# Six heads a layer turned by VectorE and a DRAM round trip in place of TensorE transposes, in a two-layer MLA and differential-attention trunk

## The reference

```python
h = rms_norm(r, norm_mix_pre[layer])
proj = h @ w_in[layer]        # q_lat, kv_lat, k_pe, dq, dk, dv, g_a, g_b
# branch A: 8 MLA heads, keys and queries 64 + 32 wide, values 64 wide
p = softmax(causal(qa @ ka.T * mla_scale))      # per head, float32
out_a = (p @ va) @ w_o_mla[layer]
# branch B: 4 differential heads, two maps each, values 128 wide
p = softmax(causal(q1 @ k1.T)) - lam * softmax(causal(q2 @ k2.T))
out_b = (rms_norm(p @ vd, diff_subln) * (1 - lam_init)) @ w_o_diff[layer]
mix = (sigmoid(g_a) * out_a + sigmoid(g_b) * out_b) @ w_out[layer]
r = r + rms_norm(mix, norm_mix_post[layer])
# then a SwiGLU feed-forward with 2,816 hidden columns, and r = r + rms_norm(ff)
```

## Time and profile before

| | |
|---|---|
| Time of three runs | 797.07 us median (796.63 to 797.28) |
| Profiled execution | 796.88 us, span 795.1 us |
| TensorE matmul busy | 787.6 us, 99% |
| VectorE, ScalarE, GpSimd busy | 575.2, 452.1, 135.8 us |
| `transposes`, L1602 | 120 matmuls, median record 273 ns |
| Attention stretches | about 94 to 158 us and 492 to 557 us of the span |

### The profile page before, as it was taken

The page is one execution under the profiler, slowest core; times in us unless marked ns, Lnnn a source line. Parts: engine busy times, 40 slices in busy tenths (PEclk is TensorE's granted clock), DMA queues, the critical chain, the costliest instruction groups (busy, mean ns, idle before and its releaser), DMA issues.

```text
span 795.1 us, 16819 instructions
## 1 busy us (share of the span) xinstructions
PE 787.6 (99%) x6300; PEld 763.7 (96%) x6300; DVE 575.2 (72%) x964; ACT 452.1 (57%) x766; POOL 135.8 (17%) x146
## 2 busy tenths in 40 slices
PE   9999999999999999999999999999999999999997
PEld 9999899999999999999999999999999999999885
DVE  6899787686787666766668987976867977676432
ACT  6657665674565444455557467566755754544331
POOL 0212000233421111101122202000433211111000
PEclk9999999999999999999999999999999999999999
DMA  9767333355266555355654674334652766657951
GB/s 335 260 219 240 129 108 105 108 182 162 57 202 216 165 169 174 119 165 169 195 174 134 197 239 149 107 106 133 181 168 77 220 212 183 193 175 197 274 134 53
DMA packets 55531, 134.87 MB, mean 170 GB/s; under 512 B 20896, under 2 KB 21536, under 8 KB 55344
## 3 DMA queue, kind: packets, MB, share of 16 engines
q1 hardware_dynamic: 38608, 131.43, 52.5%
q10 hardware_dynamic: 16864, 2.62, 1.9%
HBM read 131.93 MB, written 2.10 MB: 169 GB/s over the span
## 4 chain that ended last, share of the span: by engine, by line
PE 98%; DMA 0%; DVE 0%; ACT 0%; issue 0%; DVEq 0%
PE bank L1327 25%; PE bank L1329 24%; PE bank L1328 24%; PE bank L1361 4%; PE bank L1748 3%; PE bank L1749 3%; PE bank L1747 3%; PE bank L1352 2%; PE bank L1602 2%; PE bank L1571 2%; PE bank L1621 1%; PE bank L1420 1%; PE bank L1573 1%; PE bank L1377 1%; PE bank L1576 1%; PE bank L1381 1%
## 5 line engine op out<-in xcount | busy, mean ns | idle before, releaser
L880 DVE TENSOR_TENSOR w_lo<-w_raw,w_hi 128x1024 fp32r<-128x1024 f32 x246 | 331.0, 1348 | 37.7 <-ACT w_hi L436 34.3
L1327 PE MATMUL bank<-h_hi,w_hi 128*128 128x272 f32 (+1 forms) x1200 | 346.0, 288 | 0.0
L1329 PE MATMUL bank<-h_hi,w_lo 128*128 128x272 f32 (+1 forms) x1200 | 342.8, 286 | 0.0
L1328 PE MATMUL bank<-h_lo,w_hi 128*128 128x272 f32 (+1 forms) x1200 | 341.9, 285 | 0.0
L436 ACT ACTIVATE w_hi<-w_raw 128x1024 fp32r<-128x1024 f32 x246 | 258.9, 1056 | 121.5 <-PE bank L1329 56.4
L1327 PEld LDWEIGHTS bank<-h_hi,w_hi 128*128 128x128 f32 x1200 | 226.2, 189 | 0.5
L1329 PEld LDWEIGHTS bank<-h_hi,w_lo 128*128 128x128 f32 x1200 | 226.2, 189 | 0.0
L1328 PEld LDWEIGHTS bank<-h_lo,w_hi 128*128 128x128 f32 x1200 | 226.0, 188 | 0.0
L845 POOL TENSOR_TENSOR pbuf<-sbuf,ubuf 128x272 f32<-128x272 f32 (+1 forms) x44 | 38.4, 874 | 205.6 <-DVE ubuf L1257 204.0
L778 POOL TENSOR_TENSOR acc<-acc,sq 128x272 f32<-128x272 f32 (+1 forms) x45 | 47.5, 1055 | 137.0 <-ACT sq L449 136.8
L1257 DVE TENSOR_TENSOR ubuf<-bank,rstd_h 128x272 f32<-128x272 f32 (+1 forms) x44 | 18.9, 431 | 44.8 <-PE bank L1329 44.8
(11 more groups left out here) (238 smaller groups left out, 1234.7 us busy)
## 6 DMA issues: line engine op xcount, KB each, us to landing
w_raw<-weights SPq DMA_DIRECT2D x216, 512.0 KB, 4.0
w_raw<-weights SPq DMA_DIRECT2D x16, 384.0 KB, 3.6
w_raw<-weights SPq DMA_DIRECT2D x16, 320.0 KB, 2.9
w_first<-first_weights SPq DMA_DIRECT2D x2, 512.0 KB, 7.6
x_tok<-x_rows SPq DMA_DIRECT2D x1, 1024.0 KB, 11.3
turn<-y ACTq DMA_DIRECT2D x4, 256.0 KB, 7.2
r_tok<-turn ACTq DMA_DIRECT2D x8, 128.0 KB, 5.6
out_tokens<-o_tok SPq DMA_DIRECT2D x4, 256.0 KB, 2.0
```

Of the source, the lines that this page charges most:

```text
L880: dve.tensor_tensor(w_lo[:, n % RING, :], w_raw[:, n % RAW, :], w_hi[:, n % RING, :].bitcast(f32), ALU.subtract).then_inc(lo_ready, 1)
L1327: pe.matmul(dst, wh, hi, start=first, stop=False)
L1328: pe.matmul(dst, wh, lo, start=False, stop=False)
L1329: return pe.matmul(dst, wl, hi, start=False, stop=last)
```

## The change

`MOVED` names units 4 to 9. Their probabilities no longer go through TensorE. VectorE turns every 32 x 32 block of the 416 columns into `e_second`, right behind `probs(u)`. SP sends this in four DMAs (one for each group of 32 partitions, in pieces of 128 bytes) to the DRAM tensor `moved`, in such an order that its rows are keys and its columns queries. One unit later SP fetches what it needs in two DMAs with rows of 512 bytes into a buffer (`pt_a`, `pt_b0`, `pt_b1`: four for the units in flight), and two units later ScalarE's queue fetches the two narrow edges of 16 x 16. GpSimd zeroes the edge columns once a layer. TensorE's product of units 4 and 5 runs in step 8 in place of 6, that of 6 and 7 in step 10 in place of 8, that of 8 and 9 in `first_output_tiles`, with the halves of each handled by `hi_out` and `out_part` one step later than their product. Units 0 to 3, 10 and 11 are still transposed by TensorE.

The core of the diff:

```diff
+MOVED = range(DIFF_HEADS, UNITS - 2)
+SENDS = 4
+FETCHES = 2
@@ SP
+                def send_probs(u):
+                    sp.wait_ge(probs_turned, moved_to(l, u))
+                    to = moved_rows(l, u).rearrange("(b k) q -> k b q", k=32)
+                    for g in range(4):
+                        sp.dma_start(to[:, :, 32 * g:32 * g + 32], e_second[32 * g:32 * g + 32, u % 2, :].rearrange("p (b q) -> p b q", q=32)).then_inc(probs_sent[u % 2], 16)
+
+                def fetch_probs(u):
+                    if u == MOVED[0]:
+                        sp.wait_ge(edges_padded, l + 1)
+                    if u >= MOVED[0] + 4:
+                        sp.wait_ge(pv_ready, PRODUCTS * l + products_to(u - 4))
+                    if moved_to(l, u) > 1:
+                        sp.wait_ge(probs_landed, 16 * FETCHES * (moved_to(l, u) - 1))
+                    sp.wait_ge(probs_sent[u % 2], 16 * SENDS * pair_moved_to(l, u))
+                    p, rows = probs_of(u), moved_rows(l, u)
+                    sp.dma_start(p[:, N_META + T_B0:].rearrange("p (c q) -> p c q", c=2)[:, :, 0:P], rows[B0:B0 + 2 * P, :].rearrange("(c k) q -> k c q", c=2)).then_inc(probs_landed, 16)
+                    sp.dma_start(p[:, N_META + T_A0:N_META + T_A0 + P], rows[A0:A0 + P, :]).then_inc(probs_landed, 16)
...
+                for u in MOVED:
+                    load(at + u - MOVED[0], SLOT)
+                    send_probs(u)
+                    if u > MOVED[0]:
+                        fetch_probs(u - 1)
+                fetch_probs(MOVED[-1])
@@ ScalarE
                 def exps(u):
+                    if u - 2 in MOVED:
+                        act.wait_ge(probs_turned, moved_to(l, u - 2))
...
+                def fetch_edges(u):
...
+                    act.wait_ge(probs_sent[u % 2], 16 * SENDS * pair_moved_to(l, u))
+                    for at, row in ((T_A1, A0 + P), (T_B2, B0 + 2 * P)):
+                        act.dma_start(probs_of(u)[0:16, N_META + at:N_META + at + 16], moved_rows(l, u)[row:row + 16, P - 16:]).then_inc(edges_landed, 16)
+
                 def pt_evac(u):
-                    act.wait_ge(pt_ready, UNITS * l + u + 1)
+                    if u in MOVED:
+                        return
+                    act.wait_ge(pt_ready, turned_to(l, u))
...
-                    if u >= 2:
+                    if 2 <= u < DIFF_HEADS + 2:
                         hi_out(u - 2)
+                    elif u - 4 in MOVED:
+                        hi_out(u - 4)
                     split(S("gate") + i + HI_AHEAD)
+                    if u - 2 in MOVED:
+                        fetch_edges(u - 2)
...
+                hi_out(MOVED[-1])
                 pt_evac(UNITS - 1)
@@ VectorE
+                        if u in MOVED:
+                            after(v)
+                            dve.wait_ge(probs_ready, UNITS * l + u + 1)
+                            if u - 2 in MOVED:
+                                dve.wait_ge(probs_sent[u % 2], 16 * SENDS * pair_moved_to(l, u - 2))
+                            dve.transpose(e_second[:, u % 2, :], e[:, 0:A1]).then_inc(probs_turned, 1)
...
-                    if u >= 2:
-                        out_part(u - 2)
+                    if u - 4 in MOVED:
+                        out_part(u - 4)
...
                 dve.transpose(head_rstd[:, 0:32 * n].rearrange("p (b j) -> p b j", j=32), head_rec[:, 0:n, None].to_broadcast([P, n, 32])).then_inc(norm_bc, 1)
+                out_part(MOVED[-1])
                 out_part(UNITS - 1)
@@ TensorE
                 def pv(u):
-                    pe.wait_ge(pt_copied, UNITS * l + u + 1)
-                    if not ends_product(u):
-                        return
+                    if u in MOVED:
+                        pe.wait_ge(probs_landed, 16 * FETCHES * moved_to(l, u))
+                        pe.wait_ge(edges_landed, 16 * 2 * moved_to(l, u))
+                    else:
+                        pe.wait_ge(pt_copied, turned_to(l, u))
...
-                        if u:
+                        if 0 < u <= DIFF_HEADS:
                             pv(u - 1)
+                        elif u - 3 in MOVED and ends_product(u - 3):
+                            pv(u - 3)
                         if u == UNITS - 2:
                             head_sums()
-                        transposes(u)
+                        if u not in MOVED:
+                            transposes(u)
...
-                    for k in range(3):
+                    for k in range(2):
                         heads_ready(k)
                         for m in range(2):
                             chunk(m, k)
-                    pv(UNITS - 1)
+                    pv(MOVED[-1])
                     slot_ready(S("oa") + 1)
                     bank_free(TL("oa") + 2)
-                    for k in range(3):
+                    for k in range(2):
                         chunk(2, k)
-                    heads_ready(3)
-                    for m in range(3):
-                        chunk(m, 3)
+                    pv(UNITS - 1)
+                    for k in range(2, 4):
+                        heads_ready(k)
+                        for m in range(3):
+                            chunk(m, k)
```

More of the change, by code:

```diff
@@ L69, in first_map, with moved_to, pair_moved_to, turned_to @@
     return 2 * u if u < DIFF_HEADS else u + DIFF_HEADS
+MOVED = range(DIFF_HEADS, UNITS - 2)
+SENDS = 4
+FETCHES = 2
+def moved_to(l, u):
+    return len(MOVED) * l + u - MOVED[0] + 1
+def pair_moved_to(l, u):
+    return len(MOVED) // 2 * l + (u - MOVED[0]) // 2 + 1
+def turned_to(l, u):
+    return (UNITS - len(MOVED)) * l + (u if u < MOVED[0] else u - len(MOVED)) + 1
 def products_to(u):
@@ L240, in build_trunk @@
         (b_t,), at = place(at, [("b_t", [P, 4, TOK], f32)])
+        (pt_a,), _ = place(base + 4 * ((RAW + 2 * RING) * SLOT + GAIN_COLS + 4 * KC * TOK + 6 * TOK), [("pt_a", [P, 2, N_META + PT_COLS], f32)])
+        (pt_b0,), _ = place(lat_at + 4 * (2 * E_COLS + 2 * (N_META + PT_COLS) + 16 * UNITS), [("pt_b0", [P, N_META + PT_COLS], f32)])
+        assert _ <= lat_at + 4 * 10 * TOK
+        (pt_b1,), _ = place(lat_tmp_at + 4 * TOK, [("pt_b1", [P, N_META + PT_COLS], f32)])
+        moved = nc.dram_tensor("moved", (DEPTH * len(MOVED) * A1, P), f32).ap()
         (pm,), _ = place(lat_tmp_at, [("pm", [16, 3, 256], f32)])
@@ L315, in build_trunk @@
         probs_first = sem("probs_first")
+        probs_turned, probs_landed, edges_landed, edges_padded = (sem(n) for n in ("probs_turned", "probs_landed", "edges_landed", "edges_padded"))
+        probs_sent = [sem(f"probs_sent{i}") for i in range(2)]
         scores_ready, negmax_ready, exp_ready, probs_ready = (sem(n) for n in ("scores_ready", "negmax_ready", "exp_ready", "probs_ready"))
@@ L353, in maps_of, with probs_of, moved_rows @@
             return [(4 + u % 2, e_t[:, u % 2, :], 0)]
+        def probs_of(u):
+            if u not in MOVED:
+                return pt[:, u % 2, :]
+            return pt_a[:, u % 2, :] if (u - MOVED[0]) // 2 % 2 == 0 else (pt_b0, pt_b1)[u % 2][:, :]
+        def moved_rows(l, u):
+            return moved[(moved_to(l, u) - 1) * A1:moved_to(l, u) * A1, :]
         def T0(l):
@@ L397, in _ @@
                 end = d0 if l < DEPTH - 1 else plan.slots
+                def send_probs(u):
[14 more added lines that the diff above has]
+                    sp.dma_start(p[:, N_META + T_A0:N_META + T_A0 + P], rows[A0:A0 + P, :]).then_inc(probs_landed, 16)
+                at = plan.slot[l, "gate", 14] + MOVED[0]
+                whole = (at - first) // RING
+                with sp.Fori(0, whole) as i:
+                    for j in range(RING):
+                        load(first + j, SLOT, i, RING)
+                for n in range(first + whole * RING, at):
+                    load(n, SLOT)
+                for u in MOVED:
[4 more added lines that the diff above has]
+                fetch_probs(MOVED[-1])
+                first = at + len(MOVED)
                 whole = (end - first) // RING
@@ L471, in latent @@
                 if l and i == 0:
-                    act.wait_ge(pt_ready, UNITS * l)
+                    act.wait_ge(pt_ready, turned_to(0, UNITS - 1))
+                    act.wait_ge(probs_landed, 16 * FETCHES * moved_to(0, MOVED[-1]))
                 square(K, i if i < QC else i - QC, ps[bank_of(t)][:, c0:TOK], c0)
@@ L606, in hi_out @@
                     act.activation(am_hi[:, (u - DIFF_HEADS) // 2, t0:], ps[7][:, t0:TOK], ACT.Copy).then_inc(out_hi, 1)
+                def fetch_edges(u):
+                    if u == MOVED[0]:
+                        act.wait_ge(edges_padded, l + 1)
+                    if u >= MOVED[0] + 4:
+                        act.wait_ge(pv_ready, PRODUCTS * l + products_to(u - 4))
+                    if moved_to(l, u) > 1:
+                        act.wait_ge(edges_landed, 16 * 2 * (moved_to(l, u) - 1))
+                    act.wait_ge(probs_sent[u % 2], 16 * SENDS * pair_moved_to(l, u))
```

(32 more changed lines are left out.)

## The result

| | before | after |
|---|---|---|
| Median of 13 executions each | 796.92 us | 798.59 us |
| Lowest to highest | 796.46 to 797.48 | 796.98 to 801.55 |
| Profiled execution, its span | 796.88, 795.1 | 797.03, 795.1 |
| Mean granted clock | 0.998 in the profiled one (0.998 to 1.000 in 42 later executions) | 0.993 to 0.999 |

The ratio of the times is 1.003, 95% interval 1.0019 to 1.0041: slower, by 1.7 us at the median. The forecast was 0.3 us faster (796.6 us, 794.1 to 799.9). The median isn't the whole result. The kernel before stays within 1.0 us. The one after takes 797.0 us at best, and its times come in bunches near 798.4, 800.4 and 801.5 us, each with a lower mean clock.

A forecast was written before the change was run, and what follows sets the result against it. TensorE, busy 99% of the span, was taken to bound the kernel. Spared work, pauses and waits (-6.0 + 4.7 + 0.8 = -0.5 us) gave 796.4 us, the median 0.2 higher at 796.6 us, range 794.1 to 799.9.

The forecast's parts named there:

- TensorE spared: Attention stretch: sixty transposes go from TensorE, saving 3.0 us a layer, 6.0 us in all, up to 6.4 us.
- The pause: Ahead of the product of units 10 and 11, TensorE waits for `out_part(9)`: 2.3 us a layer, 4.7 us in all.
- VectorE's turn: Turning a 416-wide block, behind the unit's probabilities and ahead of the gate copy: 0.60 us, bounds 0.45 and 1.25 us.
- The wait at scores 8: TensorE waits for the exponentials of unit 7: 0.2 us in layer 0, 0.6 us in layer 1, together 0.8 us.
- The round trip hidden: Sends to and fetches from `moved` for unit 9, layer 1, need 8.7 us of 10.1 us before product 9.
- the late case: Rival: the round trip makes product 9 wait up to 4 us in layer 1; 804.1 us at middle values, chance 0.12.
- The sum: TensorE spared, pause and scores wait: -6.0 + 4.7 + 0.8 = -0.5 us on the profiled 796.88 us, giving 796.4.
- the clock's fall: Rival: TensorE's clock falls in the pause, 2.3 us a layer; 798.9 us for one, 801.2 for both, chance 0.12.

The follow-up runs named there:

- the long kernel: Kernel after, with one more VectorE reduction over 832 columns, its result unused, ahead of `out_part(9)`: 802.07 us, ratio 1.0067 against the kernel before.
- fill: Kernel after, with 34 small matmuls, their result unread, on TensorE ahead of the last value product: 797.06 us, ratio 1.000 against the kernel before.

## Why the prediction was wrong, step by step

- **TensorE spared, 6.0 us**: 5.6 by the table above. Right within 0.4 us.
- **The pause, 2.3 us a layer by the string root, reciprocal, wide transpose, `out_part(9)`**: right in mechanism, place and size. From product 9 to the last product was to be 159.32 - 155.10 = 4.22 us and is 155.69 - 151.49 = 4.20 us. Idle is 2.25 us and 2.2 to 2.3 us. Moving `out_part(9)` takes all of it away, which shows that the order in VectorE's queue, not the work, is the cause.
- **VectorE's turn, 0.60 us**: 0.61 us. **The wait at scores 8, 0.8 us**: 1.0 us, and the reduction in step 6 carries most of it, since its move gives 0.7 us back. The terms given for it make 10.8 - 10.1 = 0.7 us and 0.7 - 3 x 0.2 = 0.1 us where the text says 0.6 and 0.2; the sum is the same.
- **The round trip hidden**: right. TensorE never waits for it. A send was taken at 0.33 us to issue and 3.5 us to land and took 0.48 and 2.9 us at the median. The price of the late case was misread, though: the 2.9 and 6.0 us of the earlier trace rows mix the 128-byte sends into `turn` with the fetches out of it. The page of before has them apart, and with 7.2 us for the sending leg the late case would have come out 1.2 us dearer:

```profile
turn<-y ACTq DMA_DIRECT2D x4, 256.0 KB, 7.2
r_tok<-turn ACTq DMA_DIRECT2D x8, 128.0 KB, 5.6
```

  The Trainium skill wants pieces of 512 B and more for line rate ("DMA: Bandwidth & Descriptors", Specifications). Sends in 128-byte pieces cost TensorE nothing here; no run has the same sends in larger pieces, so what the small pieces cost them isn't shown.
- **The sum, -0.5 us against the profiled execution**: an execution without a fall takes 797.03 us, 0.15 us above the profiled one of before, 0.6 us off. This part of the forecast stands.
- **The failing step: the clock's fall counted at nothing in the sum, with a chance of 0.12.** It was set aside because the clock outlasts TensorE's work by 2.9 us at the end of the kernel and the pause is 2.3 us. That comparison was the error, in two ways.

A pause need not last until the fall. In the profile with one fall, TensorE's last matmul ahead of the pause ended near 153.4 and the clock fell near 156.1, 2.7 us later, when TensorE had been back at work since 155.7. Behind the pause of layer 1 in the kernel before with a pause it is 2.7 us too (557.3, 560.0), again with TensorE back at work since 559.6.

One instance at the end of the kernel was read as a limit, and it varies. In the long kernel the fall comes 3.1 us after the last matmul in layer 0 and 4.5 us in layer 1, there 1.3 us after TensorE resumed. At the end of the twelve profiled executions it comes 2.6 to 4.8 us after the last matmul. The longest is that of fill, whose matmuls end at 789.8 (columns as in the earlier trace rows):

```profile
793.00:794.00 1.00, 0.00 (x0) 0.00 (x0) 0.00 (x0) 0.00 (x0) 0.00 (x0) 1.00 1.03 383
794.00:795.00 1.00, 0.00 (x0) 0.00 (x0) 0.00 (x0) 0.00 (x0) 0.00 (x0) 0.79 0.34 127
```

Of 27 executions of the kernel after, 20 have a mean clock of 0.996 or less, the value of the profiled one with a fall, and 7 have 0.998 or more. So the rival's chance was far too low. Its price was too high: 2.3 us a fall, for 18 matmuls at the lower level, where the level came back after 3.4 us and the fall cost 1.6. With two places a kernel and 1.6 us each, the forecast would have been 798.2 us with one fall and 799.8 us with both. The median, 798.59 us, lies between the two, and its clock, 0.996, is that of one fall.

The Trainium skill ("TensorE: Matmul & The Clock Gate", What's actually happening) says that the gate's timing doesn't start anew with a kernel, and that this is why the point where the clock changes varies from run to run. The traces agree in that it varies: of two profiled executions with the same start of the product and the same 2.25 us of pause, one has a fall and one hasn't. That the cause is the one the page gives, no run here shows.

What stays open: which of the two layers falls how often; why the kernel before with its pause of 2.3 us fell in four executions of four, where the kernel after stayed up in 7 of 27; and the bunch at 801.4 to 801.6 us, 4.5 us above the undisturbed one, which is more than two falls of 1.6 us. Its mean clock, 0.993, is lower as well than the 0.994 or 0.995 of the bunch near 800.4, so the clock has a part in it, but no profile of it was taken.

## What to carry to other kernels

Before a producer is moved later, look in its engine's queue at what stands between it and the instruction that frees the consumer's buffer: here a 1.3 us transpose and what it waits for stood there. As changed, the kernel is 1.7 us slower than before; with that one line moved it is 4.0 us faster (793.08 against 797.09 us beside it). Price an idle TensorE twice, for its length and for the clock behind it, and treat a pause near the length after which the clock has once been seen to fall as a lottery, with a spread of its own, not as safe. If a pause can't be removed, idle matmuls in it are worth a try: here they cost nothing, and the clock stayed up.

## What the runs showed of the hardware

- The clock can fall after TensorE has resumed. By the mean clocks, pauses of 1.1 us had no fall in 8 executions, those of 2.3 us in 20 of 27 (4 of 4 in the kernel before with a pause), those of 3.2 us in 5 of 5. The lower level held for 3.4 us in each of the four falls in the profiles, and in the one that could be priced it cost 1.6 us.
- From TensorE's last matmul to the fall it was 2.7 to 4.5 us in the four falls behind a pause, and 2.6 to 4.8 us at the end of twelve profiled executions.
- With thirty-four 128 x 128 bf16 matmuls, 2.07 us of work, in the pause it stayed up in 11 executions of 11, on another chip than the falls seen again.
- Sends in 128-byte pieces from SBUF to DRAM, 52 KB each, landed in 2.9 us at the median; those into `turn`, 256 KB each and also in 128-byte pieces, in 7.2 us. A block-wise turn of 416 float32 columns took VectorE 0.61 us, one of 1,088 columns 1.31 us.
